# Two x tiles loaded among the modulation pieces, turnings moved inside the projections, result copies of ScalarE ahead of its modulations, first token tile in two halves

## What is computed

```python
mod = (c_act @ w_ada[l] + b_ada[l])[:, None, :]
sh1, sc1, gt1, sh2, sc2, gt2 = jnp.split(mod, N_MOD, axis=-1)
h = rmsnorm(x, g_mix[l]) * (1.0 + sc1) + sh1
proj = h @ w_in[l]
y_mla = mla_mixer(proj[..., :o1], proj[..., o1:o2], proj[..., o2:o3], positions, ...)
y_pool = pool_mixer(proj[..., o3:], w_pool[l], pool_scale[l])
x = x + gt1 * (jnp.concatenate([y_mla, y_pool], axis=-1) @ w_o[l])
```

## Time and profile before

| what | value |
|---|---|
| median of 3 runs | 1036.76 us (1036.7 to 1037.1) |
| the profiled execution, its own time | 1036.64 us |
| its span in the trace | 1034.9 us |
| busy: TensorE, VectorE, ScalarE, GpSimd | 96%, 65%, 43%, 40% of the span |
| TensorE's mean granted clock | 0.98 of full |
| HBM traffic | 159 GB/s over the span |

### The profile page before, as it was taken

The page is one execution under the profiler, slowest core; times in us unless marked ns, Lnnn a source line. Parts: engine busy times, 40 slices in busy tenths (PEclk is TensorE's granted clock), DMA queues, the critical chain, the costliest instruction groups (busy, mean ns, idle before and its releaser), DMA issues.

```text
span 1034.9 us, 12645 instructions
## 1 busy us (share of the span) xinstructions
PE 990.2 (96%) x4605; PEld 814.6 (79%) x4605; DVE 676.5 (65%) x957; ACT 447.1 (43%) x759; POOL 410.0 (40%) x306
## 2 busy tenths in 40 slices
PE   5799989999999999989999999999999999999996
PEld 0598867787888887868888888888888888888884
DVE  5848875677524689956745845844846865747766
ACT  0663247867611466532333333333234442634442
POOL 1313676599503030054643643644542300037510
PEclk9699999999899999989999999999999999999998
DMA  9903110544012242356256255355357998765523
GB/s 328 361 2 102 42 41 1 184 132 141 34 61 107 97 134 90 125 178 212 105 175 194 102 183 184 108 177 183 127 158 264 331 360 314 251 205 171 198 73 151
DMA packets 119929, 165.20 MB, mean 160 GB/s; under 512 B 8694, under 2 KB 61754, under 8 KB 119868
## 3 DMA queue, kind: packets, MB, share of 16 engines
q1 hardware_dynamic: 119868, 164.40, 47.3%
HBM read 124.26 MB, written 40.11 MB: 159 GB/s over the span
## 4 chain that ended last, share of the span: by engine, by line
PE 79%; DVE 10%; ACT 3%; POOL 2%; issue 2%; DMA 2%; SPq 2%; DVEq 0%; POOLq 0%; ACTq 0%
PE PS L2140 39%; PE PS L2174 16%; PE PS L1843 14%; PE PS L1902 4%; PE PS L2018 3%; DMA ADA<-in_w_ada 1%; POOL WIN L714 1%; PE PS L2030 1%; DVE GT L1302 1%; DVE RS L1278 1%; ACT PR L987 1%; DVE RT L1274 1%; PE PS L2090 1%; DVE XD L1817 1%; POOL ropeQ L731 1%
## 5 line engine op out<-in xcount | busy, mean ns | idle before, releaser
L2174 PE MATMUL PS<-RE 128*128 128x512 f32 x924 | 210.2, 389 | 0.0
L2174 PEld LDWEIGHTS PS<-RE 128*128 128x128 f32 x924 | 173.5, 188 | 36.4 <-issue 0.5
L1314 DVE TENSOR_TENSOR RE<-REraw,RE 128x1024 fp32r<-128x1024 f32 x77 | 106.1, 1410 | 73.9 <-ACT RE L1150 72.4
L2140 PE MATMUL PS<-HT,WS 128*128 128x512 f32 x528 | 125.5, 394 | 4.6 <-ACT U L1133 4.6
L1150 ACT ACTIVATE RE<-REraw 128x1024 fp32r<-128x1024 f32 x77 | 81.4, 1061 | 102.0 <-DMA REraw<-t_scratch 66.5
L2140 PE MATMUL PS<-HB,WS 128*128 128x512 f32 x528 | 123.3, 389 | 0.0
L2140 PEld LDWEIGHTS PS<-HT,WS 128*128 128x128 f32 x528 | 100.6, 191 | 26.1 <-issue 5.0
L2140 PEld LDWEIGHTS PS<-HB,WS 128*128 128x128 f32 x528 | 99.1, 188 | 20.6
L2140 PE MATMUL PS<-HT,W 128*128 128x512 f32 x480 | 110.8, 389 | 0.0
L2140 PEld LDWEIGHTS PS<-HT,W 128*128 128x128 f32 x480 | 89.9, 188 | 18.6
L1693 DVE TENSOR_TENSOR SG<-PS,PV 128x512 f32<-128x512 f32 x22 | 15.1, 684 | 106.5 <-PE PS L2140 96.9
(11 more groups left out here) (261 smaller groups left out, 1871.8 us busy)
## 6 DMA issues: line engine op xcount, KB each, us to landing
REraw<-h_scratch SPq DMA_DIRECT2D x77, 256.0 KB, 5.0
h_scratch<-SG SPq DMA_DIRECT2D x55, 256.0 KB, 2.4
ADA<-in_w_ada SPq DMA_DIRECT2D x12, 1024.0 KB, 8.3
TW<-in_w_down SPq DMA_DIRECT2D x22, 512.0 KB, 4.3
t_scratch<-TW SPq DMA_DIRECT2D x44, 256.0 KB, 5.0
REraw<-t_scratch SPq DMA_DIRECT2D x44, 256.0 KB, 5.1
REraw<-in_w_down SPq DMA_DIRECT2D x33, 256.0 KB, 6.6
X<-in_x SPq DMA_DIRECT2D x16, 512.0 KB, 9.1
```

The lines of the kernel that those rows point to most:

```text
L1314: dve.tensor_tensor(out_, full, hi.bitcast(F32), ALU.subtract).then_inc(ready, 1)
L2140: ins = pe.matmul(PS[:, bank, :], l, r, start=fresh and z == 0, stop=z == len(terms) - 1, skip_group_check=not fresh)
L2174: ins = pe.matmul(PS[:, D_BASE[p] + j, :], RE[e][:, a, 0, tok(j)], RE[e][:, b, 1, :], start=p in (1, 2, 7) and i == 0 and x_ == 0, stop=i ...
```

## The change

Five things are moved or split; no arithmetic of the result is changed.

1. SP loads x tiles 0 and 1 behind the second scale piece, ahead of the last two pairs of modulation pieces, and all other x tiles behind the pieces of w_in.
2. VectorE does the roots and scalings of tiles 0 and 1 between pieces 1 and 2 of the scale, and those of tiles 2 and 3 behind all four low halves of w_in. ScalarE takes the squares of tiles 0 and 1 first, and the others two at a time behind the first three modulations.
3. TensorE turns tiles 0 and 1 ahead of the column sums. Behind these it turns the identity 16 times into a bank that is overwritten later. Tile 2 is turned behind the first projection, tiles 3 to 7 in the middle of projections 1 to 5.
4. ScalarE copies out tile t-2 ahead of the modulation of tile t (before: tile t-3 behind it).
5. Tile 0 is handed on in two halves of four slices: two signals of ScalarE, two casts of GpSimd, two low halves of VectorE, two waits of TensorE. The counts of the three semaphores that are used again later grow by one.

The diff, without the shift of the three counts:

```diff
@@ -425,16 +425,15 @@
         sp.dma_start(FREQ[:], freqs.partition_broadcast(P)).then_inc(S["freq_in"], 16)
         load_sh1(1)
         load_ada(1)
+        load_x(0)
+        load_x(1)
         load_sh1(2)
         load_ada(2)
         load_sh1(3)
-        load_x(0)
         load_ada(3)
-        for t in range(1, 4):
-            load_x(t)
         for i in range(4):
             sp.dma_start(WTMraw[:, 2 * i:2 * i + 2, :], win_d[:, 2 * i:2 * i + 2, 0:TM]).then_inc(wtm_in[i], 16)
-        for t in range(4, NT):
+        for t in range(2, NT):
             load_x(t)
         sp.dma_start(GQ[:], g_q.rearrange("l n -> (l n)").partition_broadcast(P)).then_inc(S["gq_in"], 16)
         sp.dma_start(GKV[:], g_kv.rearrange("l n -> (l n)").partition_broadcast(P)).then_inc(S["gkv_in"], 16)
@@ -668,8 +667,11 @@
             pool.tensor_scalar(flat(WTM[:, HI, 2 * i:2 * i + 2, :]), flat(WTMraw[:, 2 * i:2 * i + 2, :]),
                                1.0, 0.0, ALU.mult, ALU.add).then_inc(S["wtm_hi"], 1)
 
-        for t in range(NT):
-            pool.wait_ge(S["hmod"], t + 1)
+        for k0 in (0, 4):
+            pool.wait_ge(S["hmod"], k0 // 4 + 1)
+            pool.tensor_scalar(HT[:, HI, k0:k0 + 4, tok(0)], HTf[:, k0:k0 + 4, tok(0)], 1.0, 0.0, ALU.mult, ALU.add).then_inc(S["h_hi"], 1)
+        for t in range(1, NT):
+            pool.wait_ge(S["hmod"], t + 2)
             pool.tensor_scalar(HT[:, HI, :, tok(t)], HTf[:, :, tok(t)], 1.0, 0.0, ALU.mult, ALU.add).then_inc(S["h_hi"], 1)
 
         def wu_hi(g):
@@ -874,6 +876,8 @@
             for k in range(KT):
                 last = act.activation(HTf[:, k, tok(t)], PS[:, 2 * (t % 2) + k // 4, (k % 4) * P:(k % 4 + 1) * P],
                                       ACT.Identity, scale=G1[:, k:k + 1], bias=MOD[:, k:k + 1])
+                if t == 0 and k == KT // 2 - 1:
+                    last.then_inc(S["hmod"], 1)
             last.then_inc(S["hmod"], 1)
 
         def tm_out(t):
@@ -887,18 +891,18 @@
             act.wait_ge(S["tm_out"], t + 1)
 
         squares1(0)
+        squares1(1)
 
         act.wait_ge(S["sh1_rows"], 1)
         act.activation(SHROW[0:1], PS[0:1, 4:6, :], ACT.Copy).then_inc(S["sh1_out"], 1)
-        for t in range(1, 4):
-            squares1(t)
         for t in range(NT):
+            if t >= 2:
+                tm_out(t - 2)
             modulate1(t)
-            if t < 4:
-                squares1(t + 4)
-            if t >= 3:
-                tm_out(t - 3)
-        for t in range(NT - 3, NT):
+            if t < 3:
+                squares1(2 * t + 2)
+                squares1(2 * t + 3)
+        for t in range(NT - 2, NT):
             tm_out(t)
 
         def u_out(i):
@@ -1330,11 +1334,6 @@
                 then(ins)
         dve.sem_inc(S["ang_ready"], 1)
 
-        for j in range(1, 4):
-            accumulate(j)
-        dve.wait_ge(S["rowsT"], 1)
-        dve.tensor_copy(COLS[:], PS[:, 6, 0:N_ROWS])
-
         def roots1(t0):
 
             dve.wait_ge(S["ss1"], t0 + 2)
@@ -1343,11 +1342,16 @@
             xn1(t0)
             xn1(t0 + 1)
 
-        def h_lo(t):
-            dve.wait_ge(S["h_hi"], t + 1)
-            lo(HT[:, LO, :, tok(t)], HTf[:, :, tok(t)], HT[:, HI, :, tok(t)], S["h_ready"])
-
+        def h_lo(t, k0=0, k1=KT):
+            dve.wait_ge(S["h_hi"], t + 2 if k1 == KT else 1)
+            lo(HT[:, LO, k0:k1, tok(t)], HTf[:, k0:k1, tok(t)], HT[:, HI, k0:k1, tok(t)], S["h_ready"])
+
+        accumulate(1)
         roots1(0)
+        accumulate(2)
+        dve.wait_ge(S["rowsT"], 1)
+        dve.tensor_copy(COLS[:], PS[:, 6, 0:N_ROWS])
+        accumulate(3)
 
         dve.wait_ge(S["colsum"], 2)
         dve.wait_ge(S["sh1_sum"], 1)
@@ -1355,13 +1359,14 @@
         dve.scalar_tensor_tensor(G1[:], MOD[:, 8:16], 1.0, COLS[:, ROW_MIX:ROW_MIX + 8], ALU.add, ALU.mult).then_inc(S["modcols"], 1)
 
         for i in range(4):
-            if i == 1:
-                roots1(2)
             if i == 2:
-                h_lo(0)
+                h_lo(0, 0, 4)
+            if i == 3:
+                h_lo(0, 4, KT)
             dve.wait_ge(S["wtm_hi"], i + 1)
             lo(flat(WTM[:, LO, 2 * i:2 * i + 2, :]), flat(WTMraw[:, 2 * i:2 * i + 2, :]),
                flat(WTM[:, HI, 2 * i:2 * i + 2, :]), S["wtm_ready"])
+        roots1(2)
         for t in range(1, NT):
             h_lo(t)
             if t in (1, 3):
@@ -1869,6 +1874,18 @@
                     pe.wait_ge(sh1_in[2 * ch + t // 4], 16)
                 ins = pe.matmul(PS[0:1, 4 + ch, :], CS[:, t:t + 1], ADAS[:, 2 * ch + t // 4, t % 4, :], start=(t == 0), stop=(t == KT - 1))
         ins.then_inc(S["sh1_rows"], 1)
+
+        def turn_x1(t):
+
+            pe.wait_ge(S["xn1"], t + 1)
+            if t >= 2:
+                pe.wait_ge(S["hmod"], t)
+            for k in range(KT):
+                ins = pe.transpose(PS[:, 2 * (t % 2) + k // 4, (k % 4) * P:(k % 4 + 1) * P], X[:, t, k * P:(k + 1) * P], IDENT[:])
+            ins.then_inc(S["t1"], 1)
+
+        turn_x1(0)
+        turn_x1(1)
         col_sum(0)
 
         pe.wait_ge(S["sh1_out"], 1)
@@ -1877,31 +1894,32 @@
         ins.then_inc(S["sh1_sum"], 1)
         col_sum(1)
 
-        def turn_x1(t):
-
-            pe.wait_ge(S["xn1"], t + 1)
-            if t >= 2:
-                pe.wait_ge(S["hmod"], t - 1)
-            for k in range(KT):
-                ins = pe.transpose(PS[:, 2 * (t % 2) + k // 4, (k % 4) * P:(k % 4 + 1) * P], X[:, t, k * P:(k + 1) * P], IDENT[:])
-            ins.then_inc(S["t1"], 1)
-
-
-        turn_x1(0)
-        turn_x1(1)
-        for t in range(NT):
-            if t < NT - 2:
-                turn_x1(t + 2)
-            pe.wait_ge(S["h_ready"], t + 1)
-            if t >= 2:
-                pe.wait_ge(S["tm_out"], t - 1)
-            for k in range(KT):
+        for _ in range(16):
+            pe.transpose(PS[:, 5, 0:P], IDENT[:], IDENT[:])
+
+        def project(t, k0, k1):
+            if k0 == 0:
+                pe.wait_ge(S["h_ready"], t + 2 if t else 1)
+                if t >= 2:
+                    pe.wait_ge(S["tm_out"], t - 1)
+            for k in range(k0, k1):
+                if t == 0 and k == KT // 2:
+                    pe.wait_ge(S["h_ready"], 2)
                 if t == 0 and k % 2 == 0:
                     pe.wait_ge(S["wtm_ready"], k // 2 + 1)
                 for p, (a, b) in enumerate(PASSES):
                     ins = pe.matmul(PS[:, 4 + t % 2, 0:TM], HT[:, a, k, tok(t)], WTM[:, b, k, :],
-                                    start=(k == 0 and p == 0), stop=(k == KT - 1 and p == 2))
-            ins.then_inc(S["tm_done"], 1)
+                                    start=(k == 0 and p == 0), stop=(k == KT - 1 and p == 2), skip_group_check=True)
+            if k1 == KT:
+                ins.then_inc(S["tm_done"], 1)
+
+        project(0, 0, KT)
+        turn_x1(2)
+        for t in range(1, NT):
+            project(t, 0, 4)
+            if t < NT - 2:
+                turn_x1(t + 2)
+            project(t, 4, KT)
 
         def pool_group(i):
```

More of the change, by code:

```diff
@@ L258, in hybrid_block @@
     counted_on("d_add", "tm_norm", NT)
-    counted_on("xd_part", "h_ready", NT)
-    counted_on("xd_rest", "h_hi", NT)
-    counted_on("ss3", "hmod", NT)
+    counted_on("xd_part", "h_ready", NT + 1)
+    counted_on("xd_rest", "h_hi", NT + 1)
+    counted_on("ss3", "hmod", NT + 1)
     counted_on("rs3", "kr_ready", 1)
```

## The result

The changed kernel took 1039.53 us, median of 11 runs (1037.21 to 1040.72), against 1036.36 us for the kernel before (11 runs, 1034.88 to 1037.12). The ratio is 1.0030, with a 95% interval of 1.0022 to 1.0037: slower by 3.2 us. The profiled execution took 1038.74 us, its span is 1036.9 us, its mean granted clock 0.988.

A forecast was written before the change was run, and what follows sets the result against it. TensorE's projections, then VectorE's list up to the first pooled group, were taken to bound the kernel. VectorE 3.1 us late plus 0.6 us in gate sums, 3.7 us on 1036.64 us, gave 1040.3 us, range 1036.8 to 1042.6 us.

The forecast's parts named there:

- Copies ahead of modulations: ScalarE's order ties tile t to tile t-2: 12.6 us for two tiles where TensorE needs 11.5 us.
- VectorE's list and what is late next: Behind GpSimd's last high half, VectorE 4.3 us late, less 1.2 us slack: 3.1 us; gate sums add 0.6 us.
- The sum of 3.7 us: Total lateness up to the end: 3.1 us of VectorE's list plus 0.6 us of gate sums, giving 1040.3 us.
- The meeting of gate sums with window sums: GpSimd's window sums lie 1.2 us longer over VectorE's gate sums, costing 0.6 us more.
- the 1.2 us of VectorE's wait at the latents: Wait ahead of the first latent low half, taken as all VectorE's slack and subtracted from its 4.3 us lateness.
- Piece 3 and the casts of w_in: Before the modulation columns, three GpSimd casts meet VectorE's piece 3, 0.84 us each, 2.5 us; columns at 37.7 us.
- TensorE waits there: Turnings of tiles 0 and 1, no longer behind the modulation columns, cost nothing because TensorE is waiting.
- First tile: Halves start first projection at 40.5 us; VectorE's list sets second tile at 49.6 us, covering the first at either clock.
- TensorE after the waits: TensorE idles about 1 us ahead of tiles 3 and 5, nearly 3 us ahead of tile 7, ending 1 us late.
- The casts do not meet: Rival: w_in casts miss piece 3, halves miss each other; second tile at 45.4 us, time 1035.5 us, chance 0.18.
- The late sums meet GpSimd less: Rival: moved phases save most of the 4.4 us gate sums lose at 118 to 125 us; 1036 us, chance 0.10.
- The clock stays low through the first tile: Rival: whole first tile and turning at half clock, 11.5 us; second tile 2.4 us later, 1042.7 us, chance 0.12.

The follow-up runs named there:

- experiment 1: Changed kernel with ScalarE copying out tile t-2 behind, not ahead of, the modulation of tile t: 1033.25 us, ratio 0.9973.
- experiment 2: Kernel before, with only the copy of tile t-2 put ahead of the modulation of tile t: 1041.37 us, ratio 1.0052.
- experiment 4: Changed kernel with only tile 7 modulated ahead of the copy of tile 5: 1035.56 us, ratio 0.9991.
- experiment 3: Changed kernel with gate sums of pieces 4 and 5 moved ahead of VectorE's low halves of tiles 5 and 7: 1037.68 us, ratio 1.0013.
- experiment 7: Changed kernel with the first projection waiting for both halves of its tile: 1041.48 us, ratio 1.0053.
- experiment 6: Changed kernel with 24 turnings of the identity in TensorE's wait ahead of the last projection: 1040.91 us, ratio 1.0053.
- experiment 5: Changed kernel with the edits of experiment 1 and experiment 3 together: 1031.13 us, ratio 0.9950.
- experiment 8: Kernel of experiment 5 with tile 1 turned behind the column sums and 8 turnings of the identity instead of 16: 1031.43 us, ratio 0.9959.

## Why the prediction was right

**Copies ahead of modulations.** Right in mechanism and size: a round of 12.6 us was predicted, 12.64 and 12.58 us came (49.05, 61.69, 74.27 us). Experiments 1, 2 and 4 take it away, put it alone into the old kernel, and undo its last round, and each brought the time into the range expected of it.

**VectorE's list and what is late next.** The sum of 3.7 us held, with two terms off in opposite ways. At the latents VectorE was 2.4 us late, not 3.1, mainly because GpSimd's last high half came 0.5 us ahead of my date. The meeting of gate sums with window sums then cost 1.3 us, not 0.6 (8.84 against 7.54 us). The shift of 3.7 us at the first pooled group agrees with the 134.6 us forecast because these two cancel, which is luck.

The step behind them was wrong: the 1.2 us of VectorE's wait at the latents were no slack for the first pooled group. The first gate sum ends 0.54 to 0.55 us behind the end of GpSimd's second window sum, and that window sum follows the cast of `CKV`, which was 3.73 us late. So the gate sum ended 3.73 us later (122.54 against 118.81 us), with VectorE's wait or without it. What VectorE saved by not waiting at the latents it lost again, to within 0.1 us, in its first gate sum. So the 4.3 us by which I had GpSimd's last high half late would have gone through whole, and only its coming 0.5 us earlier brought them near 3.7 us.

**Piece 3 and the casts of w_in.** A term mis-sized. I took 0.84 us for each of three meetings, 2.5 us; the piece took 4.21 us instead of 3.11, so 1.1 us in all. Two of its four sums bear that, with 1.30 us each where an undisturbed one takes 0.75 us (minimum, median and maximum in ns):

```profile
L1306 DVE SCALAR_TENSOR_TENSOR ACC<-ADA,CS,ACC x2: 1302/1304/1306, 31.6 to 32.9; 128x512 f32<-128x512 f32 x2
```

GpSimd lost time as well; its four casts:

```profile
L667 POOL TENSOR_SCALAR WTM<-WTMraw x4: 932/1180/1366, 31.3 to 35.0; 128x896 fp32r<-128x896 f32 x4
```

Taken one by one, the sum of VectorE that started 0.33 us into the first cast (31.59 against 31.26 us) ended 0.54 us behind that cast's end (32.90 against 32.36 us), and the next one 0.54 us behind the second cast's. The rule of the Trainium skill (SBUF — State Buffer, Who interferes with whom) is that the two engines exclude each other, and so the second waits until the first is done. The trace agrees with that for these two sums; what was wrong is counting a whole cast for each of three meetings, since a cast is partly over when the sum starts, and in part of the meetings it is GpSimd that waits. And this term didn't bound the columns at all. VectorE waited 2.27 us more for TensorE (36.51 us), whose list I had passed over with "TensorE waits there": behind the last shift piece it still had two turnings, 1.97 us, ahead of the column sums. The columns came at 37.1 us, 0.6 us before my date.

**First tile.** The dates were right to 0.6 us (40.40 and 49.05 us, against 40.5 and 49.6 us). The sentence that the first tile's length is covered by VectorE's list at either clock goes too far, and my own rival of a whole tile at half clock contradicts it. With its start at 40.4 us a partly slow tile was covered: in experiments 3 and 4 it took 6.94 and 6.69 us instead of 5.13, and the second tile still started at 49.04 and 49.08 us. Experiment 7 shows a tile that starts late and slows down setting the second tile's date.

**TensorE after the waits.** I had 1 us of delay for the pool groups; it was 2.1 us, since the last projection ran at half clock behind its wait. Nothing waited for it, with 1.9 us to spare: experiment 6 took the loss away and gained nothing.

**The rivals.** "The casts do not meet" was half true for piece 3, but the second tile did not come before 46.5 us, the point from which it would have decided. "The late sums meet GpSimd less" went the other way, 1.3 us more; in experiments 3, 5 and 8 they do meet it less. "The clock stays low through the first tile" did not occur in the change: 5.13 us for 24 matmuls. Where it occurred in part, in experiments 3 and 4, it cost nothing at the second tile.

**Behind the first pooled group.** The spans of the two profiled executions differ by 2.0 us only, though the first pooled group is 3.7 us late. Hardly any of that is given back by a wait of the attention stage. TensorE is still 3.6 us late at these 32 column sums, and 2.1 us late some 10 us behind them. Before, and after:

```profile
264.28 4.63 PE L2066 MATMUL PS<-ONES,MODACC 128*128 128x1 f32 x32
```
```profile
267.83 3.63 PE L2084 MATMUL PS<-ONES,MODACC 128*128 128x1 f32 x32
```

The granted clock is low for about 7 us there in the kernel before (0.67 at 266 to 268 us, 0.50 up to 272 us, 0.62 at 272 to 274 us) and for about half as long after (0.95 at 270 to 272 us, 0.50 at 272 to 274 us, 0.70 at 274 to 276 us). The change leaves the order of the instructions in this stretch as it was. The medians differ by 3.2 us, which fits: most of the 1.5 us is the clock of one execution.

## What to carry to other kernels

When an in-order engine serves both the end of one tile and the start of another, compare the whole round (here copy, modulation, cast, low half: 12.6 us for two tiles) with what the bounding engine needs for the same two tiles (11.5 us). If the round is longer, an earlier start is lost again within a few tiles; here swapping two calls was worth 6.3 us and all the rest of the change 3 us. Judge an edit at the one late row that the time follows, not at the first stage that it makes faster. And a wait of an engine is slack only if what it does next does not run into another engine's instruction that is late by as much.

## What the hardware showed that was not expected

A VectorE operation with both inputs in SBUF and a GpSimd operation that reads SBUF ran one after the other here, instruction by instruction: the sums of piece 3 beside the casts of w_in, and all four gate sums beside the window sums, where each gate sum, before and after, ended 0.53 to 0.55 us behind the end of the GpSimd instruction ahead of it. So what a meeting costs VectorE depends on how much of GpSimd's instruction is left: 0.99 us for a sum with 0.45 us left, 2.29 us for the same sum with 1.74 us left, 0.74 us with none.

TensorE's clock fell after a wait of 2.46 us between long runs of matmuls (24 matmuls in 6.58 us instead of 5.10), and not after waits of 0.7 to 1.43 us; with 24 turnings laid into the wait it did not fall. In experiment 3 it fell after 2.47 us at the same place, in experiment 7 after 2.49 and 2.31 us.

The eight one-column sums ahead of the modulation columns took 1.05 to 1.15 us in the change and in experiments 1, 3 and 4, and 1.81 to 1.87 us in experiments 5, 6 and 7, in the same code up to there. In the change's windows the clock is 1.00 at 34 to 36 us and 0.57 at 36 to 38 us, in experiment 7 it is 0.64 and 0.50, in experiment 4 it is still 1.00 in both, while PE shows busy all the time:

```profile
34.00:36.00 2.00, 2.00 (x19) 1.99 (x19) 0.24 (x1) 0.00 (x0) 1.94 (x2) 1.00 1.00 399
36.00:38.00 2.00, 2.00 (x12) 2.00 (x12) 1.21 (x3) 0.77 (x3) 0.00 (x0) 0.57 1.04 416
```

So TensorE, recorded as busy throughout, lost its clock here at a date that differs by some us between executions, and with it go 0.6 to 0.8 us of this kernel's start. The Trainium skill (TensorE: Matmul & The Clock Gate, Part 1) says that activity has to earn the fast clock. These windows neither bear that out nor refute it: the clock fell to 0.57 under a TensorE recorded as fully busy.
